# Where loads, splits and VectorE work are placed in the last two stages of a two-layer kernel

## The chip, the cores and the metric

The program runs on one core of one Trainium2 chip. The metric is device time in microseconds (us) of one launch, lower is better. The kernel before takes 2140.25 us, the median of 3 runs (2139.33 to 2142.53).

## The reference

Two layers are computed on 1024 tokens of width 1024, all in float32. The change touches only the second one:

```
p = rmsnorm(x) @ w_in                                   # twelve slices of p
y_a = (gelu(u) * spatial(layernorm(gelu(v))) * silu(z_a)) @ w_pa     # spatial: 8 masked 128x128 products
y_b = (b_g * causalconv3(c_g * x_b) * silu(z_b)) @ w_pb              # 3 taps per channel
y_c = (pool(x_c) @ w_pool * silu(z_c)) @ w_pc                        # running means over 2, 4, 8, 16 tokens, less x_c
merged = sigmoid(g_a) * y_a + sigmoid(g_b) * y_b + sigmoid(g_c) * y_c
out = rmsnorm(x + merged @ w_o)
```

## The kernel before, in words

Every float32 product is made of three passes on TensorE: the high part of the weights by the high and by the low part of the activations, and the low part of the weights by the high part. The weights come from memory into `raw` (two buffers, used in turn by the parity of the load number n), and are split there: `w_h` is a rounded copy, `w_l` is `raw - w_h`. A load into a buffer waits in `load` (L503) until the split two numbers back is done, and is issued by SyncE (SP), whose queue is an order written out by hand: an instruction that waits holds all that are behind it. All loads and stores of this part of the kernel are on that one queue.

**The 28 units** (n = 0 to 27, `UNITS`, 1291 to 1870 us). The product with `w_in` of the second layer is made in 28 units of 256 output columns, each from seven block products (a form with 7 instead of 8 products; `seventh`, 12 matmuls of 512 columns each, called o = 0 to 6). GpSimd (POOL) makes three sums of weight blocks for unit n+1 (L934, L936, L937), then seven low parts (L945); ScalarE (ACT) makes the seven high parts (`weights_high`, L1981). ACT copies the first results out of PSUM (L2022, L2025), VectorE (DVE) adds them (`from_first` L2616, `middle` L2628 to L2635, `last_sum` L2641). TensorE (PE) waits ahead of o = 4 for `from_first` of the same unit. Between these three calls DVE does the work of the branches: layer-norm statistics and rows (`normalised_rows`, 8 row tiles in units 1 to 3), window sums and `windows` for the pooling, `convolved` for the convolution. From unit 8 on, finished operands of the branches are stored to memory (`operand_out`), and the sigmoids of the gates too (`gate_out2`).

**The 12 branch blocks** (m = 0 to 11, 1870 to 2025 us). Block m multiplies operands of width 512 by 256 columns of `w_pa` (m = 0 to 3), `w_pb` (4 to 7) or `w_pc` (8 to 11): 2 x 24 matmuls of 512 columns (`branch_product`, L1592). `load_unit(NS + m)` loads its weights (0.5 MiB), POOL splits them in two halves (L857, L859), and the split waits for the end of block m-2, which used the same `w_h`. `sigmoids(m)` brings 1 MiB of gates back to `r3`, and waits for the reads of block m-2; DVE multiplies the product by them (L2845, or L2849 and L2851) and so frees PSUM for block m+2. Beside that `h_again(c)` brings the eight 0.5 MiB pieces of the first layer's result back to three buffers, ACT squares them (L2061), and POOL adds the squares up (`add_square_e`, L960): c = 1, 2 behind the split of block 3, c = 3, 4 behind that of block 4, 5, 6 behind that of block 5, and 7 behind that of block 6. `h_again(c)` for c > 3 waits for the add of c - 3.

The order on SP before, from the last unit on: operands of branch A back, `operand_out(1, ...)`, `sigmoids(0)`, `sigmoids(1)`, `gate_out2`, operands of branch B back (4 MiB), `h_again(0..2)`, and then for each m from 2: `load_unit(NS + m)`, `h_again`, at m = 6 the operands of branch C (`in2_h`, `in2_l`, 4 MiB), `sigmoids(m)`. The first two loads of `w_o` come behind `sigmoids(11)`.

**The output product** (2034 us to the end) multiplies by `w_o` in four loads N_WO to N_WO + 3 of 1 MiB; `single` splits each when the product two before it is done.

Of the kernel before, what the change touches and what calls it, by code (L numbers as in the profile page):

```python
# [74 lines left out]
def splits_before(n):  # L75

    return n - min(max(n - N_S, 0), NS)
# [77 lines left out]
def build(nc, a, out):  # L155
    ctx = ExitStack()
    with ctx:
# [208 lines left out]
        def again(count):  # L366

            return 16 + count
# [85 lines left out]
        def _(sp):  # L454
# [306 lines left out]
            for n in range(NS):  # L761
                load_unit(n + 2)
                if n == NS - 1:
                    sp.wait_ge(out_a, again(64))
                    for th in range(2):
                        sp.wait_ge(s["prod_done"], NPRE * n + 1 + th)
                        for hl in range(2):
                            dst = (act_h, act_l)[hl][:, 0:KD:2, 0:HALF] if th else tsum[0][:, :, 2 + hl, :]
                            sp.dma_start(dst.bitcast(F32),
                                         op_d[0, hl, :, :, HALF * th:HALF * th + HALF].rearrange("c p t -> p c t"))\  # L770
                              .then_inc(op_in, 16)
                if n and KIND[n - 1] == "gate":
                    gate_out2(n - 1)
                if n in SG_AT:
                    sg_store(SG_AT.index(n))
                if n in POOL_AT:
                    c = POOL_AT.index(n)
                    operand_out(2, c, 1, (2 + c % 2, c % 2), out_c, c + 1, c + 1)
                if n == UNIT_OF["u", 0, 0]:
                    sg_back(0)  # L780
                for p in range(2):
                    if n == UNIT_OF["z", 0, p] + 1:
                        operand_out(0, 2 * p, 2, (2, 0), out_a, 4 + 2 * p + 2, 4 + 2 * p + 2)
                        if p == 0:
                            sg_back(1)
                    if n == UNIT_OF["zb", 0, p] + 1:
                        operand_out(1, 2 * p, 2, (0, 2), out_b, 8 + 2 * p + 2, 8 + 2 * p + 2)
            sigmoids(0)
            sigmoids(1)
            gate_out2(NS - 1)  # L790
# [11 lines left out]
            sp.wait_ge(s["prod_done"], NPRE * NS)  # L802
            for hl in range(2):
                sp.dma_start((act_h, act_l)[hl][:, 1:KD:2, :].bitcast(F32), op_d[1, hl].rearrange("c p t -> p c t")).then_inc(op_in, 16)
            for c in range(3):
                h_again(c)
            for m in range(2, 12):
                load_unit(NS + m)
                for c in {3: (3,), 5: (4, 5), 6: (6, 7)}.get(m, ()):
                    h_again(c)  # L810
                if m == 6:
                    sp.wait_ge(s["gemm"], base_p + 8)
                    sp.wait_ge(out_c, again(128))
                    for hl, x in enumerate((in2_h, in2_l)):
                        sp.dma_start(x[:].bitcast(F32), op_d[2, hl].rearrange("c p t -> p c t")).then_inc(op_in, 16)
                sigmoids(m)
            pair_wo = [(N_WO, 1), (N_WO + 1, 0)]
            for n, k in pair_wo:
                load(n, k, "w_o_2", (n - N_WO) * NB)
            sp.wait_ge(s["m2_ready"], KD)  # L820
            for half in range(2):
                sp.dma_start(y_t[:, 4 * half:4 * half + 4, :], x2_d[4 * half:4 * half + 4].rearrange("c p t -> p c t"))\
                  .then_inc(x2_back[half], 16)
            sp.dma_start(g_row[:], a["final_g_2"].partition_broadcast(P)).then_inc(s["g_row_in"], 16)
            for n, k in pair_wo:
                load(n + 2, k, "w_o_2", (n + 2 - N_WO) * NB)

            for t in range(QB):
# [7 lines left out]
        def _(pool):  # L836
# [25 lines left out]
            def late_half_first(n):  # L862

                k = n % 2
                pool.wait_ge(w_in_[k], 16 * (n // 2 + 1))
                for half, done in ((1, s["w_half"]), (0, s["w_split"])):
                    if half == 0:
                        pool.wait_ge(s["gemm"], units_before(n - 1))
                    c = slice(half * KD // 2, (half + 1) * KD // 2)
                    nc.gpsimd.tensor_scalar(w_h[:, k, c, :], raw[:, k, c, :], 1.0, None, ALU.mult).then_inc(s["w_high"], 1)  # L870
                    pool.wait_ge(s["w_high"], 2 * n + 2 - half)
                    nc.gpsimd.tensor_tensor(w_l[:, k, c, :], raw[:, k, c, :],
                                            w_h[:, k, c, :].bitcast(F32), ALU.subtract).then_inc(done, 1)

# [88 lines left out]
            for m in range(12):  # L963
# [3 lines left out]
                split(n, n % 2, 16 * (n // 2 + 1), units_before(n - 1) if m >= 2 else None, K2)  # L967
                for c in {3: (1, 2), 4: (3, 4), 5: (5, 6), 6: (7,)}.get(m, ()):
                    add_square_e(c)
            for n in range(N_WO, N_END):  # L970
                single(n)


# [692 lines left out]
        def _(act):  # L1666
# [299 lines left out]
            def weights_high(i, o):  # L1966

                if i == NS:
                    return
                n = N_S + i  # L1970
                w = raw[:, n % 2]
                w11, w12, w21, w22 = (w[:, k:KD:2, P * h:P * h + P] for h in range(2) for k in range(2))
                src, need = ((sum2[:], 3), (w11, 0), (sum1[:], 3), (w22, 0), (w21, 3), (w12, 0), (w12, 4))[o]
                act.wait_ge(w_in_[n % 2], 16 * (n // 2 + 1))
                if need:
                    act.wait_ge(s["sum_done"], 4 * i + need)
                if i:
                    act.wait_ge(s["prod_done"], NPRE * (i - 1) + o + 1)
                else:
                    act.wait_ge(s["gemm"], units_before(N_V2) + (3 if o < 3 else 4))  # L1980
                A.activation(w7_h[:, SLOTS[o]], src, ACT.Copy).then_inc(s["w7_high"], 1)  # L1981
# [33 lines left out]

            for n in range(NS):
                kind, _, p = UNITS[n]
                weights_high(n + 1, 0)
                act.wait_ge(s["prod_done"], NPRE * n + 2)
                if n >= 2:  # L2020
                    act.wait_ge(*released(n - 2))
                A.activation(quad(n, 0), bank_of(n, "a"), ACT.Copy).then_inc(s["p_copied"], 1)  # L2022
                weights_high(n + 1, 1)
                act.wait_ge(s["prod_done"], NPRE * n + 3)
                A.activation(quad(n, 3), bank_of(n, "e"), ACT.Copy).then_inc(s["p_copied"], 1)  # L2025
# [57 lines left out]
        def _(dve):  # L2083
# [620 lines left out]
                    step(v.tensor_copy(dst[:, 0:h], src[:, 0:h]))  # L2704
                    step(v.tensor_tensor(dst[:, h:T], src[:, h:T], src[:, 0:T - h], ALU.add))

            def windows(c, levels=None):

                x, src = r3[:, c % 2, :], r3[:, 2 + c % 2, :]
                window_sums(c, range(c + 1) if levels is None else levels)  # L2710
                step(v.tensor_tensor(src[:, 0:16], src[:, 0:16], inv[:, c, :], ALU.mult))
                step(v.scalar_tensor_tensor(x[:, 16:T], src[:, 16:T], 1.0 / WINDOWS[c], x[:, 16:T], ALU.mult, ALU.subtract))
                v.tensor_tensor(x[:, 0:16], src[:, 0:16], x[:, 0:16], ALU.subtract).then_inc(s["pooled"], 1)
# [38 lines left out]
                else:  # L2752
                    step(times(n, row, i))

            def convolved(p, cg):

                dve.wait_ge(s["x_used"], units_of(("z", "zb", "cg", "bg", "zc"), UNIT_OF["cg", 0, p]))
                dve.wait_ge(s["c11_dve"], units_of(("cg", "bg"), UNIT_OF["cg", 0, p]))
                dve.wait_ge(*row_free(UNIT_OF["xb", 0, p]))
                c = 2 * p + cg  # L2760
                y, taps = r3[:, cg, :], r3[:, 2 + cg, :]
                step(v.tensor_scalar(taps, y, col_b("conv_w_2", 2 * K2 + c), col_a("conv_b_2", c), ALU.mult, ALU.add))
                for j in (1, 0):
                    d = 2 - j
                    step(v.scalar_tensor_tensor(taps[:, d:T], y[:, 0:T - d], col_b("conv_w_2", j * K2 + c), taps[:, d:T],
                                                ALU.mult, ALU.add))

            for n in range(NS):
# [14 lines left out]
                    dve.wait_ge(s["c11_act"], n - units_of(("cg", "bg"), n - 1))  # L2783
                    step(v.tensor_tensor(r3[:, 0, :], r3[:, 0, :], r3[:, 2, :], ALU.mult))
                if before == "cg":
                    convolved(UNITS[n - 1][2], 1)
                if before == "xc":
                    if UNITS[n - 1][2]:
                        window_sums(2, (0, 1))
                    else:  # L2790
                        windows(0)
                if kind == "zc" and p == 1:
                    window_sums(3, (0, 1))
# [8 lines left out]
                        x, rows = (1, (0, 2)) if before == "z" else (2, (2, 0))  # L2802
                        operands_low(4 * x + 2 * UNITS[n - 1][2] + cg + 1, rows[0] + cg, rows[1] + cg)
                if before == "cg":
                    convolved(UNITS[n - 1][2], 0)
                if before == "xc":
                    if UNITS[n - 1][2]:
                        windows(2, (2,))
                    else:
                        windows(1)  # L2810
                if kind == "zc" and p == 1:
                    windows(3, (2, 3))
                if n == 0:
                    statistics_of(range(4))
                if n in (1, 2, 3):
                    normalised_rows(range(3 * n - 3, 3 * n - 1))
                middle(n)
                if kind in ("cg", "bg"):
                    row = 0 if kind == "cg" else 2
                    if kind == "cg":  # L2820
# [6 lines left out]
                if n == 0:  # L2827
                    statistics_of(range(4, QB))
                    variance()
                if n in (1, 2):  # L2830
                    normalised_rows(range(3 * n - 1, 3 * n))
                last_sum(n)
                if kind in ("cg", "bg"):
                    multiplied(n, row, 1, last=True)
# [76 lines left out]
```

## Time and profile before

| | |
|---|---|
| median of 3 runs | 2140.25 us |
| profiled execution, its own time | 2141.03 us |
| its span, from the first to the last instruction | 2139.0 us |
| PE busy | 2070.1 us, 97% |
| POOL busy | 1200.8 us, 56% |
| DVE busy | 954.0 us, 45% |
| ACT busy | 562.4 us, 26% |
| mean granted TensorE clock | 0.985 |

The profile is one execution of 2141.03 us, 0.8 us over the median, of which the span covers 2139.0 us. PE is nearly always busy, so what can be read from such a page are the few places where it stands still, and how fast its clock was granted behind them. The span of a page's row "idle before" is the engine's own idle time; its releaser is what came last by the profile.

### The profile page before, as it was taken

The numbers are of one execution on the slowest core, as the hardware profiler recorded it, in microseconds if no ns is written. First come the engines' busy times: TensorE is split into PE (matmuls) and PEld (weight loads), VectorE is DVE, ScalarE is ACT, GpSimd is POOL, SyncE is SP. The second block draws the span as 40 slices with busy tenths as digits, with TensorE's granted clock in tenths as the row PEclk, the third lists the DMA queues.
The fourth block names the chain that finished last, engine by engine and source line by source line (L and its number), as shares of the span: only waits on it lengthen the run. The fifth ranks groups of instructions, "written<-read, shape, count | busy, mean of one in ns | idle before, by whom it ended". The sixth has DMA issues, their size and how long they took to land. (4 is left out here: it accounts for less than half of the span.)

```text
span 2139.0 us, 25832 instructions
## 1 busy us (share of the span) xinstructions
PE 2070.1 (97%) x10215; PEld 1720.3 (80%) x10215; DVE 954.0 (45%) x1270; ACT 562.4 (26%) x910; POOL 1200.8 (56%) x659
## 2 busy tenths in 40 slices
PE   6999999999999999999999999999999999969898
PEld 3888888888888888888888887788778878758778
DVE  6961355555552622222212394623463454514634
ACT  3202232333321410101102144333435423301102
POOL 2638446645363536345454347766787888737550
PEclk8999999999999999999999999999999999989999
DMA  9545544453542112111020321333323412367331
GB/s 359 132 100 148 197 142 150 144 173 99 188 177 81 40 30 69 40 50 58 20 89 20 129 80 60 99 119 105 112 76 121 154 63 96 131 255 266 118 128 80
DMA packets 173135, 251.20 MB, mean 117 GB/s; under 512 B 12296, under 2 KB 135776, under 8 KB 172000
## 3 DMA queue, kind: packets, MB, share of 16 engines
q1 hardware_dynamic: 164096, 230.78, 33.1%
q10 hardware_dynamic: 8928, 18.88, 2.3%
q8 instruction: 77, 1.26, 0.2%
q14 instruction: 34, 0.28, 0.0%
HBM read 190.66 MB, written 58.97 MB: 117 GB/s over the span
## 5 line engine op out<-in xcount | busy, mean ns | idle before, releaser
L857 POOL TENSOR_SCALAR w_h<-raw 128x1024 fp32r<-128x1024 f32 (+2 forms) x144 | 340.1, 2362 | 592.9 <-PE ps L986 268.1
L1495 PE MATMUL ps<-tb,w_h 128*128 128x512 f32 x896 | 283.9, 398 | 12.3 <-DVE quads L2616 10.1
L859 POOL TENSOR_TENSOR w_l<-raw,w_h 128x1024 fp32r<-128x1024 f32 (+2 forms) x144 | 288.5, 2003 | 12.0
L986 PE MATMUL ps<-act_h,w_h 128*128 128x512 f32 x704 | 277.1, 394 | 0.8 <-POOL w_l L859 0.4
L986 PE MATMUL ps<-act_l,w_h 128*128 128x512 f32 x704 | 275.0, 391 | 0.0
L986 PE MATMUL ps<-act_h,w_l 128*128 128x512 f32 x704 | 274.9, 391 | 0.0
L945 POOL TENSOR_TENSOR w_l<-raw,w_h 128x512 fp32r<-128x512 f32 x140 | 197.6, 1417 | 86.2 <-ACT w_h L1981 86.0
L1495 PEld LDWEIGHTS ps<-tb,w_h 128*128 128x128 f32 x896 | 168.3, 189 | 55.7 <-DVE quads L2616 13.4
L1495 PE MATMUL ps<-tb,w_l 128*128 128x512 f32 x448 | 177.3, 396 | 0.0
L986 PEld LDWEIGHTS ps<-act_h,w_h 128*128 128x128 f32 x704 | 132.8, 189 | 30.3 <-POOL w_l L859 1.4
L986 PEld LDWEIGHTS ps<-act_h,w_l 128*128 128x128 f32 x704 | 132.8, 189 | 27.9
L986 PEld LDWEIGHTS ps<-act_l,w_h 128*128 128x128 f32 x704 | 132.9, 189 | 27.7 <-issue 0.5
L1495 PE MATMUL ps<-act_l,w_h 128*128 128x512 f32 x336 | 131.4, 391 | 0.0
L1495 PE MATMUL ps<-act_h,w_h 128*128 128x512 f32 x336 | 131.4, 391 | 0.0
L1495 PE MATMUL ps<-act_h,w_l 128*128 128x512 f32 x336 | 130.7, 389 | 0.0
L1981 ACT ACTIVATE w_h<-raw 128x512 fp32r<-128x512 f32 x140 | 88.0, 628 | 159.7 <-PE ps L1495 124.9
L945 POOL TENSOR_TENSOR w_l<-sum,w_h 128x512 fp32r<-128x512 f32 x56 | 82.9, 1480 | 40.9 <-ACT w_h L1981 40.9
L2497 DVE SCALAR_TENSOR_TENSOR conv<-ps,cols_b,conv 128x1023 f32<-128x1023 f32 (+1 forms) x32 | 40.8, 1282 | 140.8 <-ACT conv L1911 138.9
L1068 PE MATMUL ps<-act_h,w_h 128*128 128x512 f32 x256 | 100.3, 392 | 0.0
L1495 PEld LDWEIGHTS ps<-tb,w_l 128*128 128x128 f32 x448 | 84.8, 189 | 19.1
L1068 PE MATMUL ps<-act_l,w_h 128*128 128x512 f32 x256 | 100.1, 391 | 0.0
L1068 PE MATMUL ps<-act_h,w_l 128*128 128x512 f32 x256 | 100.1, 391 | 0.0
(404 smaller groups left out, 4353.0 us busy)
## 6 DMA issues: line engine op xcount, KB each, us to landing
raw<-in_w_in SPq DMA_DIRECT2D x45, 1024.0 KB, 5.6
raw<-in_w_up SPq DMA_DIRECT2D x16, 1024.0 KB, 5.3
gates_scratch<-quads SPq DMA_DIRECT2D x24, 512.0 KB, 7.7
r<-gates_scratch SPq DMA_DIRECT2D x12, 1024.0 KB, 5.1
ada_lo<-in_w_ada SPq DMA_DIRECT2D x16, 512.0 KB, 3.9
ada_hi<-in_w_ada SPq DMA_DIRECT2D x16, 512.0 KB, 4.0
gates_scratch<-gate_st ACTq DMA_DIRECT2D x32, 256.0 KB, 2.0
gate_in<-gates_scratch SPq DMA_DIRECT2D x16, 512.0 KB, 4.5
```

The lines of the kernel that those rows point to most:

```text
L857: nc.gpsimd.tensor_scalar(w_h[:, k, c, :], src[:, c, :], 1.0, None, ALU.mult).then_inc(s["w_high"], 1)
L859: nc.gpsimd.tensor_tensor(w_l[:, k, c, :], src[:, c, :], w_h[:, k, c, :].bitcast(F32), ALU.subtract).then_inc(done, 1)
L945: nc.gpsimd.tensor_tensor(w7_l[:, SLOTS[o]], x, w7_h[:, SLOTS[o]].bitcast(F32), ALU.subtract)\
L986: last = nc.tensor.matmul(dst[:, tok], w[:, k, kw + c, P * cg:P * cg + P], x[:, c, tok], start=(c == 0 and p == 0), stop=(c == kc - 1 and ...
L1068: last = nc.tensor.matmul(slot(1)[:, HALF:T], w[:, n % 2, c, P * (j % 2):P * (j % 2) + P], x[:, c, tok], start=(c == 0 and p == 0), stop=( ...
L1495: last = nc.tensor.matmul(bank_of(n, bank), w[:, SLOTS[o], c, :], x(c), start=(first and c == 0 and p == 0), stop=(c == KD // 2 - 1 and p ...
L1981: A.activation(w7_h[:, SLOTS[o]], src, ACT.Copy).then_inc(s["w7_high"], 1)
L2497: ins = v.scalar_tensor_tensor(conv[:, cg, j:T], slot(cg)[:, 0:T - j], cols_b[:, bass.ds(4 * q + (at_b["w_conv"] + j * (FF // P) + c), 1)] ...
```

## The change

The loads are moved ahead by two blocks: `load_unit(NS + 2)` goes into the last unit, ahead of `operand_out(1, ...)`, `load_unit(NS + 3)` ahead of `sigmoids(0)`, and in the loop each iteration m first brings h pieces, then the sigmoids, then the weights of block m+2; at m = 10 and 11 the weights of `w_o`. The three first h pieces come in iteration 2, the operands of branch C at m = 5. The splits of the first two `w_o` loads take the later half first, which no branch block reads, with no wait for a block. ACT's copies of the two block sums wait for two of the three sums, and in unit 0 the first copy out of PSUM goes ahead of ACT's first copy for unit 1. On DVE one row tile of the layer norm, not two, stands ahead of `middle` in units 1 to 3, `windows(1)` and `windows(3)` go to the next unit, and the last tap of one convolution goes behind `from_first`.

```diff
@@ SP, units
                               .then_inc(op_in, 16)
+                    load_unit(NS + 2)
                 if n and KIND[n - 1] == "gate":
...
+            load_unit(NS + 3)
             sigmoids(0)
@@ SP, branch blocks
-            for c in range(3):
-                h_again(c)
             for m in range(2, 12):
-                load_unit(NS + m)
-                for c in {3: (3,), 5: (4, 5), 6: (6, 7)}.get(m, ()):
+                for c in {2: (0, 1, 2), 4: (3,), 5: (4, 5), 6: (6, 7)}.get(m, ()):
                     h_again(c)
-                if m == 6:
+                sigmoids(m)
+                if m == 5:
+                    sp.wait_ge(out_c, again(128))
                     sp.wait_ge(s["gemm"], base_p + 8)
-                    sp.wait_ge(out_c, again(128))
                     for hl, x in enumerate((in2_h, in2_l)):
                         sp.dma_start(x[:].bitcast(F32), op_d[2, hl].rearrange("c p t -> p c t")).then_inc(op_in, 16)
-                sigmoids(m)
-            pair_wo = [(N_WO, 1), (N_WO + 1, 0)]
-            for n, k in pair_wo:
-                load(n, k, "w_o_2", (n - N_WO) * NB)
+                if m < 10:
+                    load_unit(NS + m + 2)
+                else:
+                    load(N_WO + m - 10, m % 2 ^ 1, "w_o_2", (m - 10) * NB)
@@ POOL, w_o
-            for n in range(N_WO, N_END):
+            for n in (N_WO, N_WO + 1):
+                late_half_first(n)
+            for n in (N_WO + 2, N_WO + 3):
                 single(n)
@@ ACT
-                src, need = ((sum2[:], 3), (w11, 0), (sum1[:], 3), (w22, 0), (w21, 3), (w12, 0), (w12, 4))[o]
+                src, need = ((sum2[:], 2), (w11, 0), (sum1[:], 2), (w22, 0), (w21, 3), (w12, 0), (w12, 4))[o]
...
-                weights_high(n + 1, 0)
+                if n:
+                    weights_high(n + 1, 0)
                 act.wait_ge(s["prod_done"], NPRE * n + 2)
...
+                if n == 0:
+                    weights_high(n + 1, 0)
                 weights_high(n + 1, 1)
@@ DVE
                 if before == "cg":
-                    convolved(UNITS[n - 1][2], 1)
+                    convolved(UNITS[n - 1][2], 1, 2, 1)
...
                 if before == "cg":
-                    convolved(UNITS[n - 1][2], 0)
+                    convolved(UNITS[n - 1][2], 1, 0, 0)
+                    convolved(UNITS[n - 1][2], 0, 2, 0)
...
-                        windows(1)
+                        window_sums(1, (0, 1))
                 if kind == "zc" and p == 1:
-                    windows(3, (2, 3))
+                    window_sums(3, (2,))
+                if n in POOL_AT and POOL_AT.index(n) % 2 == 0:
+                    windows(POOL_AT.index(n) + 1)
...
                 if n in (1, 2, 3):
-                    normalised_rows(range(3 * n - 3, 3 * n - 1))
+                    normalised_rows(range(3 * n - 3, 3 * n - 2))
                 middle(n)
+                if kind == "zc" and p == 1:
+                    window_sums(3, (3,))
...
-                if n in (1, 2):
-                    normalised_rows(range(3 * n - 1, 3 * n))
+                if n in (1, 2, 3):
+                    normalised_rows(range(3 * n - 2, min(3 * n, QB)))
```

## Rows read from the trace of the kernel before

**Rows 1.** The page: busy time, share of the span and instructions of each engine.

```profile
PE 2070.1 (97%) x10215; PEld 1720.3 (80%) x10215; DVE 954.0 (45%) x1270; ACT 562.4 (26%) x910; POOL 1200.8 (56%) x659
```

**Rows 2.** Waits of PE from 1200 us on: total, times, longest.

```profile
PE ps L1592 <- POOL w_l L859: 18.3, 2, 17.6
PE ps L1495 <- DVE quads L2616: 10.1, 4, 4.7
PE ps L1016 <- POOL w_l L859: 9.0, 1, 9.0
...
PE ps L1495 <- issue: 2.0, 2, 1.1
```

**Rows 3.** Windows: us, busy PE, PEld, DVE, ACT, POOL; clock, DMA share, GB/s.

```profile
1306.00:1315.00 9.00, 9.00 (x33) 7.25 (x34) 7.78 (x14) 3.36 (x6) 5.94 (x6) 0.81 0.00 0
...
1352.00:1357.00 5.00, 5.00 (x16) 3.96 (x17) 4.89 (x4) 1.47 (x3) 4.78 (x3) 0.68 0.25 95
...
1893.00:1910.00 17.00, 0.00 (x0) 0.00 (x0) 0.89 (x1) 3.57 (x4) 5.38 (x4) 0.54 1.00 382
1910.00:1915.00 5.00, 4.86 (x11) 3.84 (x12) 0.00 (x0) 0.65 (x1) 4.83 (x5) 0.50 0.35 113
...
2025.00:2035.00 10.00, 0.97 (x4) 0.53 (x3) 9.55 (x6) 2.11 (x2) 9.83 (x5) 0.63 0.00 0
2035.00:2040.00 5.00, 5.00 (x17) 3.93 (x17) 2.67 (x2) 0.00 (x0) 4.92 (x2) 0.71 0.24 39
```

**Rows 4.** Timeline of unit 0: start, us, engine, idle before and releaser.

```profile
1302.62 1.26 POOL L937 TENSOR_TENSOR raw<-raw 128x512 f32<-128x512 f32 x1
...
1303.96 0.63 ACT L1981 ACTIVATE w_h<-sum 128x512 fp32r<-128x512 f32 x1 [5.51 <-POOL raw L937]
...
1305.93 0.73 PE L1495 MATMUL ps<-tb,w_h 128*128 128x512 f32 x2 [3.80 <-DVE quads L2616]
```

**Rows 5.** Timeline of units 1 and 2, DVE and ACT.

```profile
1336.23 1.40 DVE L2672 TENSOR_SCALAR vg<-vg,bn_mv,ln_rstd 128x512 f32<-128x512 f32 x1
...
1339.12 0.69 DVE L2628 TENSOR_TENSOR quads<-ps,quads 128x512 f32<-128x512 f32 x1
...
1349.86 0.63 ACT L1981 ACTIVATE w_h<-sum 128x512 fp32r<-128x512 f32 x1 [5.23 <-POOL raw L937]
```

**Rows 6.** Timeline of unit 9, DVE.

```profile
1507.73 1.15 DVE L2711 TENSOR_TENSOR r<-r,inv 128x16 f32<-128x16 f32 x1
...
1512.26 0.68 DVE L2628 TENSOR_TENSOR quads<-ps,quads 128x512 f32<-128x512 f32 x1
```

**Rows 7.** Timeline of the branch blocks, POOL.

```profile
1904.46 1.49 POOL L857 TENSOR_SCALAR w_h<-raw 128x512 fp32r<-128x512 f32 x1 [34.19 <-DMA raw<-in_w_pa]
...
1908.83 1.26 POOL L859 TENSOR_TENSOR w_l<-raw,w_h 128x512 fp32r<-128x512 f32 x1
...
1915.68 4.94 POOL L960 TENSOR_TENSOR h_stream<-h_stream,h_stream 128x1024 f32<-128x1024 f32 x2
...
1948.51 2.46 POOL L857 TENSOR_SCALAR w_h<-raw 128x512 fp32r<-128x512 f32 x1
```

**Rows 8.** Timeline of the branch blocks, DVE and ACT.

```profile
1880.55 1.22 DVE L2845 TENSOR_TENSOR merged<-r,ps 128x1024 f32<-128x1024 f32 x1 [9.97 <-DMA r<-gates_scratch]
...
1900.20 1.06 ACT L2061 ACTIVATE h_stream<-h_stream 128x1024 f32<-128x1024 f32 x1 [28.96 <-DMA h_stream<-x_scratch]
...
1923.70 1.22 DVE L2845 TENSOR_TENSOR merged<-r,ps 128x1024 f32<-128x1024 f32 x1 [4.22 <-PE ps L1592]
...
1934.59 1.22 DVE L2845 TENSOR_TENSOR merged<-r,ps 128x1024 f32<-128x1024 f32 x1 [4.22 <-PE ps L1592]
```

**Rows 9.** The page: DMA issues, KB each, us to landing.

```profile
r<-gates_scratch SPq DMA_DIRECT2D x12, 1024.0 KB, 5.1
```

**Rows 10.** Timeline ahead of the output product, POOL and DVE.

```profile
2022.81 3.24 POOL L857 TENSOR_SCALAR w_h<-raw 128x1024 fp32r<-128x1024 f32 x1 [14.57 <-DMA raw<-in_w_o]
...
2032.43 5.25 DVE L2859 TENSOR_TENSOR act_l<-merged,act_h 128x1024 fp32r<-128x1024 f32 x2 [0.16 <-DVE merged L2851]
```

More of the change, by code:

```diff
@@ L824, in _ @@
             sp.dma_start(g_row[:], a["final_g_2"].partition_broadcast(P)).then_inc(s["g_row_in"], 16)
-            for n, k in pair_wo:
+            for n, k in ((N_WO, 1), (N_WO + 1, 0)):
                 load(n + 2, k, "w_o_2", (n + 2 - N_WO) * NB)
@@ L870, in late_half_first @@
                     nc.gpsimd.tensor_scalar(w_h[:, k, c, :], raw[:, k, c, :], 1.0, None, ALU.mult).then_inc(s["w_high"], 1)
-                    pool.wait_ge(s["w_high"], 2 * n + 2 - half)
+                    pool.wait_ge(s["w_high"], 2 * splits_before(n) + 2 - half)
                     nc.gpsimd.tensor_tensor(w_l[:, k, c, :], raw[:, k, c, :],
@@ L2705, in window_sums, with windows @@
                     step(v.tensor_tensor(dst[:, h:T], src[:, h:T], src[:, 0:T - h], ALU.add))
-            def windows(c, levels=None):
+            def windows(c):
                 x, src = r3[:, c % 2, :], r3[:, 2 + c % 2, :]
-                window_sums(c, range(c + 1) if levels is None else levels)
                 step(v.tensor_tensor(src[:, 0:16], src[:, 0:16], inv[:, c, :], ALU.mult))
@@ L2753, in multiplied, with convolved @@
                     step(times(n, row, i))
-            def convolved(p, cg):
+            def convolved(p, cg, first, last):
                 dve.wait_ge(s["x_used"], units_of(("z", "zb", "cg", "bg", "zc"), UNIT_OF["cg", 0, p]))
@@ L2761, in convolved @@
                 y, taps = r3[:, cg, :], r3[:, 2 + cg, :]
-                step(v.tensor_scalar(taps, y, col_b("conv_w_2", 2 * K2 + c), col_a("conv_b_2", c), ALU.mult, ALU.add))
-                for j in (1, 0):
+                if first == CONV - 1:
+                    step(v.tensor_scalar(taps, y, col_b("conv_w_2", 2 * K2 + c), col_a("conv_b_2", c), ALU.mult, ALU.add))
+                for j in range(min(first, CONV - 2), last - 1, -1):
                     d = 2 - j
@@ L2790, in _ @@
                     else:
+                        window_sums(0, (0,))
                         windows(0)
@@ L2804, in _ @@
                 if before == "cg":
-                    convolved(UNITS[n - 1][2], 0)
+                    convolved(UNITS[n - 1][2], 1, 0, 0)
+                    convolved(UNITS[n - 1][2], 0, 2, 0)
                 if before == "xc":
                     if UNITS[n - 1][2]:
-                        windows(2, (2,))
+                        window_sums(2, (2,))
+                        windows(2)
                     else:
-                        windows(1)
+                        window_sums(1, (0, 1))
                 if kind == "zc" and p == 1:
-                    windows(3, (2, 3))
+                    window_sums(3, (2,))
+                if n in POOL_AT and POOL_AT.index(n) % 2 == 0:
+                    windows(POOL_AT.index(n) + 1)
                 if n == 0:
```

## The prediction, made before the changed kernel was run

> **What bounds the kernel now.** I read the page first: TensorE is busy for 97% of the span [rows 1], so time can only be won where it stands still or runs at the lower clock. The view of its waits in the stretch that the change touches gives a short list [rows 2]: 18.3 us in the branch blocks, 17.6 of them one wait ahead of block 2; 9.0 us ahead of the output product; 10.1 us in four waits inside the units, all for `from_first`; 2.0 us in two waits that carry no releaser. Sum: 39.4 us. The windows show the second price of a stall [rows 3]. Behind the wait of 3.80 us in unit 0 the granted clock is 0.81 of full for 9 us and 33 matmuls start; at 0.233 us each it would be 38.5, so 5.5 x 0.233 = 1.3 us are lost. Behind the 4.7 us wait 16 start in 5 us instead of 21.4: 1.3 us. Behind the 17.6 us wait the clock is 0.50, that is the lower level of 1.2 GHz: 11 start instead of 22, 2.4 us lost. Behind the 9.0 us wait 17 instead of 22 (and more in the fraction of a microsecond ahead of the window): 1.5 us. Together 6.5 us, so at most 46 us can be had.
>
> **The units.** Unit 0: ACT's copy for unit 1 waits for POOL's third sum, which ends at 1303.9, and only then does ACT take the first result out of PSUM, which VectorE needs [rows 4]. With the copies swapped that result goes out at 1298.5, VectorE is done before TensorE stops at 1302.1, and 3.80 + 1.3 us go. What is late next, ACT's copy for unit 1, is needed only when unit 1 begins, 8 us later. The 4.7 us wait of unit 2 has a longer chain: two row tiles of about 2.9 us each (1336.23 to 1339.12) hold `middle` of unit 1, that holds ACT's sigmoids, they hold the last high part for unit 2, that holds POOL's sums for unit 3, and ACT is again released by the third sum at 1349.86 [rows 5]. The change takes one tile out (2.9 us) and one sum (1.3 us), 4.2 of 4.7 us; what is left, about 0.5 us, I take at 0.6, and the clock loss of 1.3 goes, since a wait of 0.7 us ahead of block 0 is followed by none. The tile itself goes behind `middle`, where VectorE has some 6 us before `last_sum`; if POOL slows it, up to 2 us come back. The two convolution waits (10.1 - 3.8 - 4.7 = 1.6 us) end on the same copy by ACT and on three long VectorE operations ahead of `from_first`; the earlier sum alone gives 1.3 us for each 0.8. The two unnamed waits (2.0 us) are in units 10 and 14: `windows(1)` holds `middle` of unit 9 from 1507.7 to 1512.3 [rows 6], 4.6 us, and the pooling result is late by 1.1 us at most. Moved, it costs VectorE the same 4.6 us in unit 10, ahead of a `middle` that nobody waits for until some 10 us later; I cost it at nothing. Sum of the units: 10.1 + 2.0 - 0.6 + 2.6 = 14.1 us, bounds 8 (the wait in unit 2 stays with its clock loss) and 14.7.
>
> **The branch blocks.** A half block is 5.45 us ((1934.59 - 1923.70) / 2 [rows 8]), a block 10.9. POOL ends the split that block 2 waits for at 1910.1, 17.6 us after block 1's end at 1892.5; unstalled, blocks 3, 4, 5 begin at 1903.4, 1914.3, 1925.2. All times below are on the scale of the trace before. The load for block 2 now goes out when the split of block 0 is done, and the one for block 3 while the last stores land; both splits (5.6 us, 1904.46 to 1910.1 [rows 7]) end long before they are needed. 17.6 + 2.4 us go at this place. But DMA runs at 382 GB/s here [rows 3], so 0.5 MiB takes 1.37 us, and the load ahead of the stores makes everything behind it about 1.3 us late: the gates of block 0 at 1881.9 instead of 1880.55 (harmless, TensorE needs PSUM again at 1892.5), the h pieces 0, 1, 2 at 1901.5, 1902.8, 1904.1 instead of 1900.2 and on [rows 8].
>
> What is late next is POOL. Its adds for pieces 1 and 2 stand behind the split of block 3 and ahead of the split of block 4. They can begin when ACT has squared piece 1 (1902.8 + 1.1 = 1904), take 4.9 us [rows 7], and the split of block 4 then runs from 1908.9 to 1914.5: block 4 is 0.2 late, I say 0.5. Then the new order bites. `h_again(4)` is now behind the load for block 6, and that waits for the split of block 4 (before, it stood behind the load for block 5, which waits for the split of block 3). Piece 4 is thus issued at 1915.0, with 0.5 MiB ahead of it. A free transfer of 1 MiB lands after 5.1 us [rows 9], 2.7 of them movement, so piece 4 needs 2 x 1.37 + 2.4 = 5.1 us, plus 1.1 for the square, 2.5 to 3.4 for the add, and 5.6 to 7.6 for the split (a copy takes 2.46 instead of 1.49 us where VectorE adds two SBUF operands [rows 7]). The split of block 5 ends at 1915.0 + 5.1 + 1.1 + 2.9 + 6.1 = 1930.2, 4.9 us after block 4's end at 1925.4. The same for block 6, worse by the transfers: the 4 MiB of branch C (11 us) are now issued at 1917, ahead of pieces 6 and 7, which go out at 1930.7 and land about 1937; square, add and split end at 1937 + 1.1 + 2.9 + 6.1 = 1947.1, while block 5 (with 1.3 us clock loss) ends at 1930.2 + 12.2 = 1942.4: 4.7 us. By block 7 POOL has one add and a split inside a block of 12.2 us, and no more is lost. So the blocks give 17.6 + 2.4 + 0.5 (small waits of blocks 6 and 7 before, where VectorE's reads are 0.2 to 0.3 us late) - 0.5 - 4.9 - 4.7 - 2.6 = 7.8 us. Bounds: 20 if the pieces come in time, and 1 if both splits take the slow value and the clock loss is 2.4 twice.
>
> The Trainium skill, page "DMA: Bandwidth & Descriptors", section "Anatomy of one DMA — SWDGE (gpsimd) path", gives about 2.0 us fixed and bytes at 436 GB/s. An estimate by it puts piece 4 at 4.4 instead of 5.1 us and would make the sum 1.4 us better over the two stalls; the measured landing decides for me. A rule that speaks against this change is in the page "TensorE: Matmul & The Clock Gate", section "HAM oscillation — how this bites in real kernels": waits repeated at each tile can throttle TensorE anew each time. The trace agrees so far as its stalls of 3.8 us and more were all followed by a dip.
>
> **The output product.** The first load of `w_o` waits in the queue for reads of block 9 and lands at 2022.6, then POOL takes 12 us for the whole split [rows 10], while TensorE is through with block 11 at 2025.6. Now it is issued behind `sigmoids(10)` and the split of block 10, at about 1998, and its later half is split right behind that of block 11 (ends 2008) in 6.1 us, the earlier half behind block 10's end (2014.7) by 2020.9: 4.7 us to spare. The second load keeps its issue time and is split by 2035; TensorE wants it at 2025.6 + 21.8 = 2047.4. The activations could be the next wait: the last `act_l` ends at 2037.7 [rows 10], and the piece is used 19 us after the start, at 2044.6. The third load lands near 2055 behind 4 MiB of `y_t`, is split by 2066, and is wanted at 2069. All covered: 9.0 + 1.5 = 10.5 us, bounds 7 and 10.6.
>
> **Sum.** 14.1 + 7.8 + 10.5 = 32.4 us. The profiled execution took 2141.03 us, so 2108.6; the median is 0.8 lower, 2107.8. A difference under 0.2% (4.3 us) could not be told from none.
>
> **Rivals.** *A, the h pieces do not hold POOL*: if pieces 4 and 6 land as early as the blocks allow, all 20 us are kept: 2140.25 - 14.1 - 20 - 10.5 = 2095.6. For it: POOL has slack on average, 6 splits and 7 adds are 51 us in 65 us of blocks. Against it: the order on the queue, which no speed changes. *B, unit 2 keeps its stall* because the tiles run at the slowed rate of the rows around 1352: 2107.8 + 6 = 2114. *C, the branch blocks give nothing net*, the change not doing what it says: the early loads only move the wait to blocks 4 to 6, with a dip behind each: 2107.8 + 7.8 = 2116. *D, slower*: the clock does not come back between the two new stalls. At 1.2 GHz a block takes 20.5 instead of 10.9 us; the 32.4 us are used up after 65 us at the lower level, more than three blocks; from there it is slower than before, with six such blocks 2107.8 + 58 = 2166. Against it: every dip in the trace ended within 5 us of work.
>
> **How the numbers follow.** The forecast has 0.56, with 2102 to 2113 as its own range (its stalls at 3.5 and 7 us each, the unit wait 0 to 2). A has 0.15, B 0.12, C 0.11, D 0.03; 0.03 is left for several gains missing at once, which ends near no change. The time is 2108. The range goes from A to C, 2095 to 2117. Faster 0.95, within 0.2% 0.02, slower 0.03.
>
> **What would show it.** Right: no wait over 1 us inside the units; none ahead of block 2; waits of TensorE on `w_l` (L859) ahead of blocks 5 and 6, 4 to 5 us each, with POOL's adds released by ACT's squares and those by transfers of h; no wait ahead of the output product. Wrong: blocks 5 and 6 unstalled (A), a wait of over 3 us for `from_first` in unit 2 (B), one ahead of blocks 2 to 4 of several us (C), or a clock below 0.8 over whole blocks (D).

## The result, and the profile after

The changed kernel takes 2107.64 us, the median of 4 runs (2105.1 to 2108.22), against 2139.79 us before (4 runs). The ratio over all runs is 0.9846, with a 95% interval of 0.9829 to 0.9863 (the two medians alone give 0.9850). The forecast was 2108 us with a range of 2095 to 2117. The profiled execution of the changed kernel took 2108.0 us, its span is 2106.2 us. Line numbers in it are a few higher than before: L1594 is the branch block product, L1497 the one of the units, L2621 is `from_first`, L2066 the squares, L2025 the first copy out of PSUM, L1983 `weights_high`, L2012 the sigmoids, L2633 `middle`.

The waits of TensorE in the changed kernel, from 1190 us on, answer to [rows 2]: engine and line, what it waited for, total, times, longest.

```profile
PE ps L1594 <- POOL w_l L859: 10.3, 3, 6.0
...
PE ps L1497 <- DVE quads L2621: 1.8, 1, 1.8
```

The 17.6 us wait, the 9.0 us wait, three of the four waits for `from_first` and both without a releaser are gone. In their place two waits stand on the same line as the first (the third is the half microsecond ahead of block 0). The timeline of PE gives their places, ahead of blocks 5 and 6, and that of the wait left in unit 2:

```profile
1341.81 0.74 PE L1497 MATMUL ps<-tb,w_h 128*128 128x512 f32 x2 [1.76 <-DVE quads L2621]
...
1913.17 0.64 PE L1594 MATMUL ps<-act_h,w_h 128*128 128x512 f32 x1 [3.76 <-POOL w_l L859]
...
1931.98 0.79 PE L1594 MATMUL ps<-act_h,w_h 128*128 128x512 f32 x1 [6.03 <-POOL w_l L859]
```

Windows behind each of the three answer to [rows 3]; the clock is the number ahead of the DMA share:

```profile
1341.00:1350.00 9.00, 8.19 (x29) 6.54 (x30) 8.49 (x10) 3.28 (x7) 7.80 (x5) 0.81 0.19 69
...
1913.00:1918.00 5.00, 4.83 (x14) 3.83 (x15) 0.00 (x0) 0.00 (x0) 2.44 (x2) 0.66 1.04 396
...
1932.00:1937.00 5.00, 5.00 (x12) 3.94 (x13) 0.00 (x0) 0.00 (x0) 4.92 (x3) 0.50 0.76 283
```

At 0.227 us each (22 starts in 5 us, as [rows 3] were read) the second lost 1.8 us and the third 2.3; the first, with 29 starts in 8.2 us of work instead of 35, lost 1.4.

The chain behind the wait ahead of block 5, in the timelines of POOL, SP and ACT. The split of block 4 ends at 1897.8 and releases the load for block 6; only behind that go pieces 4 and 5; piece 4 is there at 1902.8, and POOL has stood 3.63 us for it:

```profile
1896.51 1.29 POOL L859 TENSOR_TENSOR w_l<-raw,w_h 128x512 fp32r<-128x512 f32 x1
1897.86 2.40 POOL L960 TENSOR_TENSOR h_stream<-h_stream,h_stream 128x1024 f32<-128x1024 f32 x1
...
1897.90 0.37 SPq L504 DMA_DIRECT2D raw<-in_w_pb  x1
1898.32 0.97 SPq L800 DMA_DIRECT2D h_stream<-x_scratch  x2
...
1902.76 1.06 ACT L2066 ACTIVATE h_stream<-h_stream 128x1024 f32<-128x1024 f32 x1 [4.97 <-DMA h_stream<-x_scratch]
...
1903.89 2.41 POOL L960 TENSOR_TENSOR h_stream<-h_stream,h_stream 128x1024 f32<-128x1024 f32 x1 [3.63 <-ACT h_stream L2066]
1906.27 2.47 POOL L857 TENSOR_SCALAR w_h<-raw 128x512 fp32r<-128x512 f32 x1
```

The same one block later, with the 4 MiB of branch C issued at 1900.4 ahead of pieces 6 and 7: piece 6, issued at 1913.7, is squared at 1921.1, 7.4 us later instead of 4.4, and POOL stands 6.76 us.

```profile
1900.42 0.41 SPq L815 DMA_DIRECT2D in_h<-operand_scratch  x1
...
1913.66 0.97 SPq L800 DMA_DIRECT2D h_stream<-x_scratch  x2
...
1921.07 1.06 ACT L2066 ACTIVATE h_stream<-h_stream 128x1024 f32<-128x1024 f32 x1 [15.29 <-DMA h_stream<-x_scratch]
...
1922.21 3.14 POOL L960 TENSOR_TENSOR h_stream<-h_stream,h_stream 128x1024 f32<-128x1024 f32 x1 [6.76 <-ACT h_stream L2066]
```

The first split of `w_o`, which answers to [rows 10]. The later half (1986.2) follows the split of block 11 at once, the earlier one the end of block 10, and both are done at 1998.9, while the output product begins at 2003.5:

```profile
1984.73 1.54 POOL L859 TENSOR_TENSOR w_l<-raw,w_h 128x512 fp32r<-128x512 f32 x1
1986.23 3.75 POOL L870 TENSOR_SCALAR w_h<-raw 128x1024 fp32r<-128x1024 f32 x1
...
1992.87 3.32 POOL L870 TENSOR_SCALAR w_h<-raw 128x1024 fp32r<-128x1024 f32 x1 [0.40 <-PE ps L1594]
1996.27 2.66 POOL L872 TENSOR_TENSOR w_l<-raw,w_h 128x1024 fp32r<-128x1024 f32 x1
```

All kernels are compared by stages as well, cut at the first matmul of unit 0, of block 0 and of the output product, each from one profiled execution. "Blocks" holds the wait ahead of the output product too. The part ahead of unit 0 is the same code in all and lies between 1287.9 and 1291.4 us, so the times of whole runs scatter more than the stages. Where kernels share the code of a stage, its time repeats within 1.7 us in the units (564.0 to 565.7 in five kernels), 0.2 us in the blocks (163.9 to 164.1 in four) and 1.1 us in the output product (104.3 to 105.4 in five). The profiled executions of blocks_only, units_vector, plain_split and operands_later were 3.3 to 4.1 us slower than the medians of those kernels, so their spans are not to be compared with medians.

| kernel | ahead of unit 0 | units | blocks | output product | span |
|---|---|---|---|---|---|
| before | 1291.0 | 579.6 | 164.1 | 104.3 | 2139.0 |
| changed | 1289.5 | 565.3 | 148.7 | 102.7 | 2106.2 |
| blocks_only | 1291.1 | 580.6 | 158.9 | 105.1 | 2135.7 |
| units_only | 1289.3 | 565.7 | 163.9 | 104.5 | 2123.4 |
| out_only | 1289.5 | 579.3 | 154.4 | 103.6 | 2126.8 |
| units_scalar | 1287.9 | 568.2 | 164.1 | 104.4 | 2124.6 |
| units_vector | 1291.1 | 575.5 | 164.1 | 105.4 | 2136.1 |
| tile_behind | 1288.0 | 561.8 | 148.9 | 103.1 | 2101.8 |
| plain_split | 1291.4 | 565.3 | 150.1 | 103.7 | 2110.5 |
| operands_later | 1290.9 | 565.6 | 145.5 | 103.0 | 2105.0 |
| pieces_early | 1289.3 | 564.0 | 136.6 | 103.3 | 2093.2 |
| both | 1289.5 | 562.0 | 136.9 | 102.7 | 2091.1 |

Of the 32.8 us of span, 14.3 are in the units, 15.4 in the blocks with the wait behind them, 1.6 in the output product and 1.5 ahead of it all, where nothing was changed. The 9.0 us of the wait are in the second of these, so the blocks themselves gave 15.4 - 9.0 = 6.4 us.

### The profile page after: what moved, and what is told of

Its sections match the earlier page's. It is cut to its first block, busy times and chain, and to the rows that moved or that the text cites. A ratio compares the mean times of both kernels' runs of the same rounds, so it can differ in the third digit from the quotient of the medians.

```text
span 2106.2 us, 25837 instructions
## 1 busy us (share of the span) xinstructions
PE 2064.4 (98%) x10215; PEld 1719.2 (82%) x10215; DVE 958.6 (46%) x1270; ACT 564.1 (27%) x910; POOL 1201.1 (57%) x659
## 4 chain that ended last, share of the span: by engine, by line
PE 90%; POOL 3%; DMA 3%; DVE 1%; issue 1%; SPq 1%; ACT 0%; DVEq 0%; POOLq 0%; ACTq 0%
PE ps L988 32%; PE ps L1497 25%; PE ps L1070 8%; PE ps L1018 7%; PE ps L1594 3%; PE ps L1281 3%; PE ps L1028 2%; PE ps L1242 2%; PE ps L1451 2%; DMA ada_w<-in_w_ada 1%; PE ps L1256 1%; POOL w_h L857 1%; POOL w_l L859 1%; PE ps L1643 1%; DMA h_stream<-x_scratch 1%
## 5 line engine op out<-in xcount | busy, mean ns | idle before, releaser
L857 POOL TENSOR_SCALAR w_h<-raw 128x1024 fp32r<-128x1024 f32 (+2 forms) x140 | 325.8, 2327 | 559.6 <-PE ps L988 268.1
L859 POOL TENSOR_TENSOR w_l<-raw,w_h 128x1024 fp32r<-128x1024 f32 (+2 forms) x140 | 279.4, 1996 | 11.7
L1497 PE MATMUL ps<-tb,w_h 128*128 128x512 f32 x896 | 281.8, 396 | 1.8 <-DVE quads L2621 1.8
L945 POOL TENSOR_TENSOR w_l<-raw,w_h 128x512 fp32r<-128x512 f32 x140 | 204.0, 1461 | 88.8 <-ACT w_h L1983 88.6
L1497 PEld LDWEIGHTS ps<-tb,w_h 128*128 128x128 f32 x896 | 168.2, 188 | 42.2 <-issue 2.6
L1497 PE MATMUL ps<-tb,w_l 128*128 128x512 f32 x448 | 176.9, 395 | 0.0
L1983 ACT ACTIVATE w_h<-raw 128x512 fp32r<-128x512 f32 x140 | 87.9, 629 | 182.1 <-PE ps L1497 141.4
L1497 PE MATMUL ps<-act_l,w_h 128*128 128x512 f32 x336 | 131.5, 391 | 0.0
L1497 PE MATMUL ps<-act_h,w_h 128*128 128x512 f32 x336 | 131.4, 391 | 0.0
L1497 PE MATMUL ps<-act_h,w_l 128*128 128x512 f32 x336 | 130.7, 389 | 0.0
L1497 PEld LDWEIGHTS ps<-tb,w_l 128*128 128x128 f32 x448 | 84.4, 188 | 18.9
```

Of the source, the lines that this page charges most:

```text
L857: nc.gpsimd.tensor_scalar(w_h[:, k, c, :], src[:, c, :], 1.0, None, ALU.mult).then_inc(s["w_high"], 1)
L859: nc.gpsimd.tensor_tensor(w_l[:, k, c, :], src[:, c, :], w_h[:, k, c, :].bitcast(F32), ALU.subtract).then_inc(done, 1)
L945: nc.gpsimd.tensor_tensor(w7_l[:, SLOTS[o]], x, w7_h[:, SLOTS[o]].bitcast(F32), ALU.subtract)\
L1497: last = nc.tensor.matmul(bank_of(n, bank), w[:, SLOTS[o], c, :], x(c), start=(first and c == 0 and p == 0), stop=(c == KD // 2 - 1 and p ...
```

## The experiments

**The three parts alone.** *blocks_only* is the kernel before with the new queue order for the blocks, *units_only* with the ScalarE and VectorE edits, *out_only* with the `w_o` loads and splits. Only the parts of the change's own diff that belong to each were applied; where blocks_only differs from the changed kernel's queue is

```diff
 (changed kernel -> blocks_only)
                 if m < 10:
                     load_unit(NS + m + 2)
-                else:
-                    load(N_WO + m - 10, m % 2 ^ 1, "w_o_2", (m - 10) * NB)
+            for n, k in ((N_WO, 1), (N_WO + 1, 0)):
+                load(n, k, "w_o_2", (n - N_WO) * NB)
...
-            for n in (N_WO, N_WO + 1):
-                late_half_first(n)
-            for n in (N_WO + 2, N_WO + 3):
+            for n in range(N_WO, N_END):
                 single(n)
```

and out_only against the kernel before, but for the way a list and a semaphore count are written, is

```diff
                 sigmoids(m)
-            pair_wo = [(N_WO, 1), (N_WO + 1, 0)]
-            for n, k in pair_wo:
-                load(n, k, "w_o_2", (n - N_WO) * NB)
+                if m >= 10:
+                    load(N_WO + m - 10, m % 2 ^ 1, "w_o_2", (m - 10) * NB)
...
-            for n in range(N_WO, N_END):
+            for n in (N_WO, N_WO + 1):
+                late_half_first(n)
+            for n in (N_WO + 2, N_WO + 3):
                 single(n)
```

> The kernel before with the new queue order of the branch blocks alone; units and output product as before. Additive theory, by the stage times read from the two traces: first branch block to last one 155.0 us before and 148.7 after, so 6 us faster than before (range 4 to 8), with waits of about 4 and 6 us ahead of blocks 5 and 6 and the 9 us wait ahead of the output product still there. Rival, the stages interact (TensorE early in the units moves the transfers): blocks alone gain under 3 or over 10 us.

> The kernel before with the ScalarE and VectorE edits of the units alone. Additive theory: the 28 units took 579.6 us before and 565.3 after, so 14 us faster (12 to 16), with the 17.6 us wait ahead of block 2 unchanged. Rival: units gain less because the transfers behind them set the start of the blocks; under 10 us.

> The kernel before with the early loads of w_o and the split of the later half first alone. Theory: the 9.0 us wait goes with its 1.5 us of clock loss, 10.5 us faster (9 to 11.5). Rival, activations instead of weights release the output product next: a wait on VectorE of 2 us or more stays and the gain is under 8.

Measured, beside 2140.45 us for the kernel before: blocks_only 2134.14 us, ratio 0.9965 (0.9951 to 0.9979), 6.3 us; units_only 2125.17 us, 0.9924 (0.9907 to 0.9941), 15.3 us; out_only 2129.1 us, 0.9946 (0.9929 to 0.9962), 11.4 us. The sum is 32.9 us, each part known to some 3 to 4 us. The changed kernel is 32.2 us below the kernel before timed beside it, and 2140.45 - 2107.64 = 32.8 us below the median used here: the parts add up as far as these times can tell. The stages say it more closely. The units give 13.9 us in units_only against 14.3 in the changed kernel, and the blocks with the wait behind them 5.2 us in blocks_only and 9.7 in out_only, together 14.9 against 15.4. (Of the 9.7 us, 0.5 come with a shorter wait ahead of block 2, 16.8 instead of 17.6 us, ahead of everything that out_only changes; in the five traces that have this wait it lies between 16.8 and 17.7 us.) The waits of blocks_only show the old ones of the units and of the output product untouched, and the new pair of the blocks already there:

```profile
PE ps L1495 <- DVE quads L2616: 10.1, 4, 4.7
PE ps L1592 <- POOL w_l L859: 10.1, 3, 6.0
PE ps L1016 <- POOL w_l L859: 9.0, 1, 9.0
```

So the waits ahead of blocks 5 and 6 come from the queue order alone, not from a TensorE that is early.

**Do late h pieces cause them?** *pieces_early* moves the pieces ahead of the load that waits:

```diff
-                for c in {2: (0, 1, 2), 4: (3,), 5: (4, 5), 6: (6, 7)}.get(m, ()):
+                for c in {2: (0, 1, 2), 4: (3, 4, 5), 5: (6, 7)}.get(m, ()):
                     h_again(c)
```

> The changed kernel with h pieces 4 and 5 issued in iteration 4 and pieces 6 and 7 in iteration 5, ahead of the gates and the operands of branch C. Theory, the waits of 3.8 and 6.0 us ahead of blocks 5 and 6 come from the late pieces: both go with their clock losses (14 starts in 5 us instead of 22 behind the first, 12 behind the second, 1.8 and 2.3 us), 13 to 14 us faster than the changed kernel, about 2094. Rival, POOL's work itself is too much for these blocks (adds and splits are 10.5 to 12.5 us in a block of 10.9): waits of 1 to 3 us on the split of w_l stay ahead of blocks 5, 6 and 7, with adds that wait for nothing, and under 8 us are won.

Measured: 2095.66 us (2094.13 to 2097.2), ratio 0.979 (0.9774 to 0.9806) to the kernel before; the blocks fall from 148.7 to 136.6 us, by 12.1. Its waits, and POOL's adds of pieces 3 to 6, none of which has idle time ahead of it:

```profile
PE ps L1594 <- POOL w_l L859: 2.4, 3, 1.2
```

```profile
1896.80 4.95 POOL L960 TENSOR_TENSOR h_stream<-h_stream,h_stream 128x1024 f32<-128x1024 f32 x2
1901.72 1.49 POOL L857 TENSOR_SCALAR w_h<-raw 128x512 fp32r<-128x512 f32 x1
...
1908.36 5.72 POOL L960 TENSOR_TENSOR h_stream<-h_stream,h_stream 128x1024 f32<-128x1024 f32 x2
1914.06 1.48 POOL L857 TENSOR_SCALAR w_h<-raw 128x512 fp32r<-128x512 f32 x1
```

The late pieces were the cause of 9.8 - 1.7 = 8.1 us of waiting (0.5 and 1.2 us remain ahead of blocks 5 and 6), and 12.1 - 8.1 = 4.0 us more come back with the clock, close to the 1.8 + 2.3 us read from the windows. The rival fails by its own numbers, since over 8 us were won and block 7 has no wait, but it names what remains: POOL's own adds and splits, back to back from 1896.8 to 1930. From the first add to the end of the split they take 11.6 us for block 5 and 12.4 for block 6, while TensorE needs 10.9 for a block, so they do not quite fit.

**Which of the two delays holds block 6?** *operands_later* keeps the pieces in the place of the changed kernel and moves the 4 MiB of branch C behind pieces 6 and 7:

```diff
-                if m == 5:
+                if m == 6:
                     sp.wait_ge(out_c, again(128))
```

> The changed kernel with the operands of branch C (4 MiB) loaded in iteration 6, behind h pieces 6 and 7, instead of iteration 5. Theory: the wait ahead of block 5 stays at about 3.8 us; that ahead of block 6 falls from 6.0 to about 2.5 us, since pieces 6 and 7 then have only 0.5 MiB ahead of them, 3 to 4 us faster. Rival, the 4 MiB do not matter and only the place behind the load for block 7 does: the wait stays at 5 us or more.

Measured: 2102.72 us, ratio 0.9824 (0.9809 to 0.9839) to before; blocks 145.5 us, 3.2 less than the changed kernel. The two waits:

```profile
1914.86 0.79 PE L1594 MATMUL ps<-act_h,w_h 128*128 128x512 f32 x1 [3.76 <-POOL w_l L859]
...
1931.35 0.50 PE L1594 MATMUL ps<-act_h,w_h 128*128 128x512 f32 x1 [3.76 <-POOL w_l L859]
```

The wait ahead of block 6 fell from 6.03 to 3.76 us, not to 2.5: the 4 MiB account for 2.3 us of it. The rest goes with the place behind the load for block 7, as pieces_early shows, down to the 1.2 us of POOL's own work. The stage still fell by the forecast 3 to 4 us, because 0.9 us of clock loss went as well. (The median is 4.9 us under the changed kernel's, which was timed in another job.)

**Which engine's edits free the units?** *units_scalar* has the two ScalarE edits alone on the kernel before, *units_vector* the VectorE edits alone (each as in the diff of the change).

> The kernel before with the two ScalarE edits alone (two sums instead of three; in unit 0 the first copy out of PSUM ahead). Theory: unit 0's wait and its clock loss go (3.8 + 1.3), the wait of unit 2 falls by the one sum of 1.3 to about 3.4, the two waits in the convolution units go: 8 to 9 us of the 14.3 in the units. Rival, the VectorE edits do most of the work: under 5 us.

> The kernel before with the VectorE edits alone. Theory: the two unnamed waits of units 10 and 14 go (2 to 2.7 us), the wait of unit 2 falls by a row tile of 2.9 to about 1.8 with its dip, the 3.8 us wait of unit 0 stays with its dip, and the waits of the convolution units stay at about 0.8 each, since VectorE sat idle ahead of its first sum there: 5 to 6 us. Rival, the last tap held the first sum: the convolution waits go here.

Measured: units_scalar 2126.75 us, ratio 0.9937 (0.992 to 0.9954), units 568.2 us, 11.4 less than before; units_vector 2133.93 us, 0.997 (0.996 to 0.9981), units 575.5 us, 4.1 less. Their waits within the units, ScalarE edits first:

```profile
PE ps L1495 <- DVE quads L2619: 3.5, 1, 3.5
```

```profile
PE ps L1495 <- DVE quads L2616: 8.6, 4, 3.8
```

With ScalarE's edits alone only the wait of unit 2 remains, 1.2 us shorter: the one sum. It won only 0.2 us there, since the clock behind it was lower (12 starts in the next 5 us, against 16 in [rows 3]). The waits without releaser in units 10 and 14 are gone as well, which I had given to VectorE's edits; either kernel is without them. VectorE's edits alone leave 3.84 us in unit 0 and 3.00 us in unit 2 (1.7 less, not 2.9), and 1.8 us in two more waits. These two are not the ones from before: those stood in units 21 and 25, where the last tap of the convolution was taken from ahead of the first sum, and the new ones of 0.91 and 0.90 us stand one unit later, in 22 and 26. The place of the tap did hold the first sum, as the rival said, but by way of POOL: its third sum for the next unit took 2.27 us, 1.29 with the tap gone, and ACT's copies wait for that sum. First before, then units_vector, then the new wait:

```profile
1739.58 2.27 POOL L937 TENSOR_TENSOR raw<-raw 128x512 f32<-128x512 f32 x1
...
1736.21 1.29 POOL L937 TENSOR_TENSOR raw<-raw 128x512 f32<-128x512 f32 x1
...
1760.00 0.73 PE L1495 MATMUL ps<-tb,w_h 128*128 128x512 f32 x2 [0.91 <-DVE quads L2616]
```

Units 21 and 22 together took 39.9 us before, 39.7 here and 38.5 without a wait: alone, the moved tap shifts the wait to the next unit, and only with ScalarE's edits beside it do all of these waits go. By the stages the first of my two sums, 8 to 9 us, was too low (11.4). The second, 5 to 6 us, is not decided: the stage gives 4.1, in an execution 4.0 us over the median and with a heavier clock loss behind unit 0, and the medians give 6.4. The two stages sum to 15.5 against 14.3 together, since both kernels remove the waits of units 10 and 14.

**The wait that is left in unit 2.** *tile_behind* takes the last row tile from ahead of `middle` in unit 1:

```diff
-                if n in (1, 2, 3):
-                    normalised_rows(range(3 * n - 3, 3 * n - 2))
+                if n in (2, 3):
+                    normalised_rows(range(3 * n - 4, 3 * n - 3))
                 middle(n)
...
-                    normalised_rows(range(3 * n - 2, min(3 * n, QB)))
+                    normalised_rows(range(max(3 * n - 3, 0), 3 * n - 1))
```

> The changed kernel with no row tile of the layer norm ahead of middle in unit 1 (tiles 0 and 1 behind it, one tile ahead and two behind in units 2 and 3). Theory: the 1.8 us wait of unit 2 is what the remaining tile (3.0 us) still holds back through middle, ScalarE and POOL's sums; it goes with its dip (29 starts in 9 us instead of 35), 3 us faster than the changed kernel in the units. Rival, POOL's chain for unit 3 is the bound by itself (sums slowed by VectorE's rows): the wait stays over 1 us.

Measured: 2104.92 us, ratio 0.9837 (0.9821 to 0.9853) to before; units 561.8 us, 3.5 less than in the changed kernel (unit 2 alone fell from 22.9 to 19.3 us), and no wait of TensorE of any length that the view lists is left in the units. The tile was what held it, by way of the sigmoids. The whole time (2.7 us under the changed kernel's, which was timed in another job) agrees but could not show it by itself.

**The order of halves.** *plain_split* is the changed kernel with its early `w_o` loads and `single` for all four splits, that is with the second part of the diff of blocks_only.

> The changed kernel with the first two w_o splits in plain order, each half behind the end of block 10 or 11, and the early loads kept. Theory: POOL's 12.2 us for a whole split begin at the end of block 10, 10.9 us ahead of the output product, so a wait of 1 to 2 us comes ahead of it and the changed kernel's time grows by 1 to 2 us: of the 9 us the early load gives at least 7.5, the order of halves the rest. Rival, the order of halves carries the gain: a wait of 5 us or more.

Measured: 2108.94 us, ratio 0.9851 (0.9835 to 0.9868); blocks with the wait 150.1 us, 1.4 more than in the changed kernel.

```profile
2006.81 0.50 PE L1016 MATMUL ps<-act_h,w_h 128*128 128x512 f32 x1 [1.51 <-POOL w_l L859]
```

The early load is worth 7.5 of the 9.0 us, the order of halves 1.5.

**The two together.** *both* has the edits of pieces_early and tile_behind.

> The changed kernel with both the early h pieces and no row tile ahead of middle in unit 1. If the two are independent: the 12 us of the first and some 3 of the second, about 2093; the only waits of TensorE over 0.3 us from unit 0 on are three small ones ahead of blocks. Rival, the clock or POOL takes one of them back: no faster than the first alone (2095.7).

Measured: 2092.88 us, the median of 5 runs (2091.61 to 2093.15), beside 2139.54 before; ratio 0.9779 (0.9765 to 0.9792). That is the fastest version, 47 us under the kernel before and 15 under the changed one (which was timed in another job). Over pieces_early the units give 2.0 us more and not 3.5, because the wait of unit 2 had no clock loss behind it there (last section). From unit 0 on the view of TensorE's waits lists 2.5 us in three places ahead of blocks, the longest 1.2 us, and none in the units.

## Why the prediction was right

*Units* (14.1 us, measured 14.3). The step on unit 0 held: the wait and its dip are gone. The step on unit 2 named the right chain and a wait of 0.6 us that would carry no dip; it is 1.76 us with 1.4 us lost, and unit 2 gave 2.9 us of a forecast 5.4. The mis-sized term is "the change takes one tile out (2.9 us)": removing the tile alone shortened the wait by 1.7 us (units_vector). The last low part of POOL starts 2.9 us earlier there, but the three operations from it to the first sum for unit 3 then run beside the tiles and take 1.52, 1.54 and 1.74 us instead of 1.29, 1.09 and 1.30. The other side of the balance is in unit 0, which gave 5.6 us (forecast 5.1), and in the later units: by the times of `last_sum` in the two traces, which are 10.0 us apart in unit 8, 12.7 in units 14 to 16 and 15.6 in unit 27, the pooling units gave 2.7 us (forecast 2.0) and the convolution units 2.9 (forecast 1.6). The waits that I read were those of the matmuls alone, while the weight loads of the same places had stood 1.2 us rather than 0.8, and 0.8 of the 2.9 us are in units 22 and 26, where the list shows no wait at all (19.65 us long before, 19.25 after). Two errors cancelled here. To give the waits of units 10 and 14 to `windows(1)` was half the story: an earlier sum removes them too.

*Branch blocks* (7.8 us, measured 6.4). Each step held in kind: nothing ahead of blocks 2, 3 and 4, then block 5 and block 6, with the chain of load, pieces, square, add and split as written. The wait ahead of block 5 was forecast at 4.9 (its own times give 4.8) and is 3.76 us: block 4 was not late at all, so the piece was issued 0.6 us sooner beside it, and piece 4 landed after 4.4, not 5.1 us. That is what the estimate by the Trainium skill's page "DMA: Bandwidth & Descriptors", section "Anatomy of one DMA — SWDGE (gpsimd) path", had given (4.4 us), and for this term it was the nearer one, in part by luck. Its fit is stated for transfers that GpSimd issues, and SyncE issued this one; 1 MiB of gates with nothing ahead of it took 4.8 to 5.0 us in the same trace, not 4.4. What shortened the term is that the piece was issued 0.42 us behind the load ahead of it, and that this lone load of 0.5 MiB landed after 3.35 us, which leaves 2.0 us beside 1.37 of movement where I had taken 2.4. The wait ahead of block 6 was forecast at 4.7 and is 6.03 us, piece 6 taking 7.4 instead of 6.3 us to its square. The clock was under-priced, 1.3 us each against 1.8 and 2.3. It is this term that brings the sum down to 6.4; the two waits together, 9.8 us, are close to the forecast 9.6.

*Output product* (10.5 us). The changed kernel starts it without a wait, and its part of the span fell by 1.6 us with the clock: 9.0 + 1.6 = 10.6 us. out_only shows it alone (11.4 us), plain_split how little of it hangs on the order of halves.

*The rivals.* A (2095.6 us) did not come by itself, but pieces_early made it so on purpose and landed at 2095.66 us: the condition was the order on the queue, as written. That the figures agree is luck as well, since 1.7 us of waiting stayed in the blocks and unit 2 lost its clock dip, which A does not contain. B came in part, the wait in unit 2 at 1.8 instead of 4.7 us. C and D did not occur; the lowest clock read in the changed kernel's windows was 0.50, for 5 us. (D was priced with a block of 20.5 us at the lower clock; its row, 11 starts in 5 us, gives 21.8.) 1.5 us of the span's fall are ahead of unit 0, where the kernels are alike, so the hit to a few tenths of a microsecond is partly luck; the stages carry the claim, not the total.

## What to carry to other kernels

When a load that waits is moved forward in a queue written by hand, list what has come to stand behind its wait and who needs that next: here 20 us were won at one place and 14 lost again at two others, by small transfers that nobody had thought of as urgent, and one changed line gave 12 of them back. Read a stall with the clock behind it: the stalls of 3 to 6 us in these traces made their unit or block 1.4 to 3.0 us longer than the wait itself. Moving work to another place can move the wait with it, as the tap did from unit 21 to unit 22: look one unit further. Check a forecast by stages, since the whole can be right by errors that cancel.

## What the runs showed of the hardware that was not expected

What the clock takes back behind a stall depends on more than its length. The same wait of unit 0 cost differently in two kernels: 3.80 us, then 33 starts in the 9 us window [rows 3], and in units_vector 3.84 us, then 29 starts, at a granted clock of 0.72 instead of 0.81:

```profile
1306.00:1315.00 9.00, 8.94 (x29) 7.19 (x30) 6.82 (x13) 2.68 (x6) 5.25 (x6) 0.72 0.00 0
```

The wait of unit 2, 4.72 us before and 4.74 us in blocks_only with the same code, had 16 starts in 5 us behind it [rows 3], and then 12 at the lower level of 1.2 GHz; the unit took 25.8 and 27.0 us:

```profile
1352.00:1357.00 5.00, 4.97 (x12) 3.91 (x13) 4.89 (x4) 1.20 (x3) 4.95 (x4) 0.50 0.29 109
```

A wait of only 1.76 us (unit 2 of the changed kernel) had a dip to 0.81 behind it, while one of 1.16 us ahead of block 6 in pieces_early and one of 1.51 us in plain_split had none, as the windows behind them show, pieces_early first. It is not the length that divides them: in pieces_early the wait of unit 2 is 1.77 us too, with the same code in the units, and there the clock stayed at full, with 36 starts in the same 9 us where the changed kernel had 29 (third line). Unit 2 took 21.3 us in it, and 22.8 to 22.9 in the four other kernels with these units:

```profile
1921.00:1926.00 5.00, 5.00 (x23) 4.08 (x23) 3.17 (x1) 0.00 (x0) 4.92 (x3) 1.00 0.71 208
```

```profile
2006.00:2011.00 5.00, 4.19 (x18) 3.49 (x19) 4.97 (x4) 0.00 (x0) 4.92 (x3) 1.00 0.02 3
```

```profile
1341.00:1350.00 9.00, 8.33 (x36) 6.84 (x37) 8.72 (x9) 4.74 (x9) 9.00 (x6) 1.00 0.18 63
```

What decides between them was not tried. So a stall of this length could not have been priced to better than 1.6 us from its length alone.
